# Key marks for four tokens an operation, and gates spread by two fp32r products, in a hybrid layer on one core

## The reference, cut to what matters

```python
def peer_block(h, w_query, sub_keys, expert_u, expert_v):
    ...
    cand_i = top_i[:, :, 0, :, None] * PEER_N_KEYS + top_i[:, :, 1, None, :]
    best_s, best_j = lax.top_k(cand_s.reshape(t, PEER_HEADS, PEER_TOPK * PEER_TOPK), PEER_TOPK)
    expert_idx = jnp.take_along_axis(cand_i.reshape(...), best_j, axis=-1)
    gate = jax.nn.softmax(best_s, axis=-1)
    act = jax.nn.gelu(jnp.einsum('td,thkd->thk', h, expert_u[expert_idx]), approximate=False)
    coef = (gate * act).astype(h.dtype)
    return jnp.einsum('thk,thkd->td', coef, expert_v[expert_idx])
```

## Time and profile before

| | |
|---|---|
| median of 3 runs | 3032.3 us (3028.78 to 3032.59) |
| the profiled execution's own time | 3030.53 us |
| its span in the trace | 3028.7 us |
| mean granted clock of TensorE | 0.932 of 2.4 GHz |
| PE busy | 2806.0 us, 93% |
| DVE busy | 1431.3 us, 47% |
| ACT busy | 911.8 us, 30% |
| POOL busy | 963.5 us, 32% |

### The profile page before, as it was taken

How to read it: one execution, slowest core, us unless ns; L and a number is a source line. 1 busy time by engine, 2 the same in 40 slices (tenths; PEclk the granted TensorE clock), 3 DMA queues, 4 the chain that set the end, 5 groups by cost and what they waited for, 6 DMA issues and landing times.

```text
span 3028.7 us, 41491 instructions
## 1 busy us (share of the span) xinstructions
PE 2806.0 (93%) x14216; PEld 2388.0 (79%) x14216; DVE 1431.3 (47%) x3468; ACT 911.8 (30%) x1205; POOL 963.5 (32%) x425
## 2 busy tenths in 40 slices
PE   8798898898899999769998999999999999999996
PEld 7688788788888677558877788888877888888885
DVE  2465565565565211244496677777502222222223
ACT  1412212212212132233332355545423222222221
POOL 0312302302302134324443333333344444444441
PEclk9897897897797999979999999999999999999998
DMA  4201101101100132213344345554665555555561
GB/s 184 71 28 42 55 14 42 55 17 38 55 28 28 56 111 90 91 60 111 111 131 129 104 160 176 208 169 160 215 207 180 183 181 200 180 188 193 174 203 53
DMA packets 130237, 354.27 MB, mean 117 GB/s; under 512 B 10640, under 2 KB 43536, under 8 KB 128784
## 3 DMA queue, kind: packets, MB, share of 16 engines
q1 hardware_dynamic: 127648, 312.76, 31.4%
q10 hardware_dynamic: 2544, 40.90, 3.5%
HBM read 284.41 MB, written 69.21 MB: 117 GB/s over the span
## 4 chain that ended last, share of the span: by engine, by line
issue 41%; PE 34%; POOL 17%; DVE 5%; ACT 2%; POOLq 0%; DMA 0%; DVEq 0%; SPq 0%; ACTq 0%
POOL w_lo L829 17%; PE bank L1355 5%; PE bank L466 4%; PE bank L467 4%; PE bank L468 4%; PE bank L1471 2%; DVE cv L1003 2%; PE bank L1486 2%; PE bank L1479 2%; PE bank L1414 1%; PE bank L1404 1%; PE bank L1595 1%; PE bank L1514 1%; PE bank L1446 1%; PE bank L1521 1%
## 5 line engine op out<-in xcount | busy, mean ns | idle before, releaser
L829 POOL TENSOR_TENSOR w_lo<-raw,w_hi 128x1024 fp32r<-128x1024 f32 x344 | 847.5, 2465 | 1768.1 <-ACT w_hi L698 868.8
L466 PE MATMUL bank<-lat_hi,w_hi 128*128 128x512 f32 x1568 | 631.8, 403 | 22.1 <-DMA sk<-sub_keys 8.0
L468 PE MATMUL bank<-lat_hi,w_lo 128*128 128x512 f32 x1568 | 615.1, 392 | 0.0
L467 PE MATMUL bank<-lat_lo,w_hi 128*128 128x512 f32 x1568 | 615.0, 392 | 0.0
L466 PE MATMUL bank<-c_hi,w_hi 128*128 128x512 f32 x1024 | 404.3, 395 | 7.0 <-ACT gu L755 7.0
L467 PE MATMUL bank<-c_lo,w_hi 128*128 128x512 f32 x1024 | 404.2, 395 | 0.0
L468 PE MATMUL bank<-c_hi,w_lo 128*128 128x512 f32 x1024 | 404.0, 395 | 0.0
L466 PEld LDWEIGHTS bank<-lat_hi,w_hi 128*128 128x128 f32 x1568 | 297.8, 190 | 82.1 <-issue 24.0
L468 PEld LDWEIGHTS bank<-lat_hi,w_lo 128*128 128x128 f32 x1568 | 296.8, 189 | 64.6
L467 PEld LDWEIGHTS bank<-lat_lo,w_hi 128*128 128x128 f32 x1568 | 297.7, 190 | 56.6
L1308 DVE TENSOR_SCALAR oh<-cst,eidT 128x128 f32<-128x128 f32 x512 | 242.6, 474 | 104.5 <-PE bank L1700 102.6
(11 more groups left out here) (283 smaller groups left out, 3572.6 us busy)
## 6 DMA issues: line engine op xcount, KB each, us to landing
raw<-w SPq DMA_DIRECT2D x344, 512.0 KB, 3.7
gu_dram<-gu SPq DMA_DIRECT2D x128, 256.0 KB, 3.9
g_dram<-gs ACTq DMA_DIRECT2D x8, 4096.0 KB, 12.4
gl<-gu_dram SPq DMA_DIRECT2D x32, 1024.0 KB, 6.8
gq<-g_dram SPq DMA_DIRECT2D x32, 1024.0 KB, 9.3
ada<-w_ada SPq DMA_DIRECT2D x32, 512.0 KB, 3.7
ada_a<-w_ada SPq DMA_DIRECT2D x12, 512.0 KB, 10.8
xin<-x SPq DMA_DIRECT2D x4, 512.0 KB, 12.4
```

Source lines behind the costliest of these rows:

```text
L466: nc.tensor.matmul(out, hi, rh, start=start, stop=False)
L467: nc.tensor.matmul(out, hi, rl, start=False, stop=False)
L468: return nc.tensor.matmul(out, lo, rh, start=False, stop=stop)
L829: nc.gpsimd.tensor_sub(w_lo[:, slot, :], raw[:, slot % RAW, :], w_hi[:, slot, :].bitcast(F32)).then_inc(split_done, 1)
```

## The change

The `oh` buffer becomes four: `oh_i` (marks of the first key, fp32r), `oh_j` (marks of the second key), `oh_h` (those marks times the gate's high part, fp32r) and `oh_l` (times the gate's low part, fp32r). Each has two buffers of four tokens. ACT makes the high part of all gates once (`g_hi`), and DVE subtracts it from row 2 of `eidT`. DVE makes the marks by tensor_tensor over four tokens at once. ACT multiplies by the high part, one activation with a scale for each token. PE does two fp32r products for a token in place of one fp32 product. DVE waits for each buffer by itself. ACT's copy out of the bank writes `gs` with the tokens innermost. ACT's outer loop has one turn less, and its last turn is written out.

```diff
-        oh = gates("oh", [2, 4, 2, P])
+        oh_i = gates("oh_i", [2, 4, P], F32R)
+        oh_h = gates("oh_h", [2, 4, P], F32R)
+        oh_l = gates("oh_l", [2, 4, P], F32R)
+        oh_j = gates("oh_j", [2, 4, P])
+        g_hi = gates("g_hi", [SEQ], F32R)
...
+            act.wait_ge(e_ev, LAT)
+            nc.scalar.copy(g_hi[:, :], eidT[:, 2, :]).then_inc(gh_done, 1)
+            def high_gates(n, group, z):
+                act.wait_ge(oh_second, n + (group + 1))
+                for v in range(4):
+                    nc.scalar.activation(oh_h[:, z, v, :], oh_j[:, z, v, :], ACT.Copy,
+                                         scale=g_hi[:, bass.ds(n * 4 + (4 * group + v), 1)].bitcast(F32)).then_inc(oh_high, 1)
+            act.wait_ge(gh_done, 1)
+            high_gates(0, 0, 0)
+            def gate_quarter(i, j, t, last):
+                for w in range(4):
+                    for z in range(2):
+                        n = i * (2 * GTOK // 4) + t * 8
+                        if not (last and w == 3 and z == 1):
+                            high_gates(n, j * GTOK // 4 + 2 * w + z + 1, 1 - z)
+                        act.wait_ge(g_mm, n + (j * GTOK // 4 + 2 * w + z + 1))
+                        nc.scalar.copy(gs[:, j, :, bass.ds(t * 32 + (8 * w + 4 * z), 4)],
+                                       bank[z][:, :].rearrange("p (t i) -> p i t", t=4)).then_inc(g_ev, 1)
...
-                                act.wait_ge(g_mm, i * (2 * GTOK // 4) + t * 8 + (j * GTOK // 4 + 2 * w + z + 1))
-                                nc.scalar.copy(gs[:, j, :, bass.ds(t * 32 + (8 * w + 4 * z), 4)].rearrange("p i t -> p t i"),
-                                               bank[z][:, :].rearrange("p (t i) -> p t i", t=4)).then_inc(g_ev, 1)
...
-            dve.wait_ge(e_ev, LAT)
-            with dve.Fori(0, SEQ // 8) as t:
+            dve.wait_ge(gh_done, 1)
+            g_lo = eidT[:, 2, :]
+            nc.vector.tensor_sub(g_lo, g_lo, g_hi[:, :].bitcast(F32)).then_inc(glo_done, 1)
+            dve.wait_ge(glo_done, 1)
+            def marks(t, z):
+                cols = bass.ds(t * 8 + 4 * z, 4)
+                nc.vector.tensor_tensor(oh_j[:, z, :, :], rep(iota, 4), bc(eidT[:, 1, cols], P), ALU.is_equal).then_inc(oh_second, 1)
+                nc.vector.tensor_tensor(oh_i[:, z, :, :], rep(iota, 4), bc(eidT[:, 0, cols], P), ALU.is_equal).then_inc(oh_first, 1)
+                dve.wait_ge(oh_second, t * 2 + (z + 1))
+                nc.vector.tensor_tensor(oh_l[:, z, :, :], oh_j[:, z, :, :], bc(eidT[:, 2, cols], P), ALU.mult).then_inc(oh_low, 1)
+            def marks_free(t, z):
+                dve.wait_ge(g_mm, t * 2 + (z + 1))
+                dve.wait_ge(oh_high, t * 8 + (4 * z + 4))
+                dve.wait_ge(oh_low, t * 2 + (z + 1))
+            for z in range(2):
+                marks(0, z)
+            with dve.Fori(0, SEQ // 8 - 1) as t:
                 for z in range(2):
-                    dve.wait_ge(g_mm, t * 2)
-                    for w in range(4):
-                        col = bass.ds(t * 8 + (4 * z + w), 1)
-                        first_ = oh[:, z, w, 0, :]
-                        nc.vector.tensor_scalar(first_, iota, eidT[:, 0, col], None, ALU.is_equal).then_inc(oh_done, 1)
-                        nc.vector.tensor_scalar(oh[:, z, w, 1, :], iota, eidT[:, 1, col], eidT[:, 2, col],
-                                                ALU.is_equal, ALU.mult).then_inc(oh_done, 1)
+                    marks_free(t, z)
+                    marks(t + 1, z)
...
-                        pe.wait_ge(oh_done, i * 64 + (16 * w + 8 * z + 8))
+                        pe.wait_ge(oh_high, i * 32 + (8 * w + 4 * z + 4))
+                        pe.wait_ge(oh_low, i * 8 + (2 * w + z + 1))
+                        pe.wait_ge(oh_first, i * 8 + (2 * w + z + 1))
...
-                            last = mm(bank[z][:, v * P:(v + 1) * P], oh[:, z, v, 1, :], oh[:, z, v, 0, :],
-                                      start=True, stop=True)
+                            out = bank[z][:, v * P:(v + 1) * P]
+                            mm(out, oh_h[:, z, v, :], oh_i[:, z, v, :], start=True, stop=False)
+                            last = mm(out, oh_l[:, z, v, :], oh_i[:, z, v, :], start=False, stop=True)
```

More of the change, by code:

```diff
@@ L413, in layer_kernel @@
         e_ev = sem("e_ev")
-        oh_done = sem("oh_done")
+        oh_first = sem("oh_first")
+        oh_second = sem("oh_second")
+        oh_high = sem("oh_high")
+        oh_low = sem("oh_low")
+        gh_done = sem("gh_done")
+        glo_done = sem("glo_done")
         g_mm = sem("g_mm")
@@ L776, in _, with gate_store @@
                 nc.scalar.copy(eidT[:, :, bass.ds(b * P, P)], bank[4][:, 0:3 * P].rearrange("p (a b) -> p a b", a=3)).then_inc(e_ev, 1)
-            with act.Fori(0, SEQ // GTOK // 2) as i:
+            act.wait_ge(e_ev, LAT)
[16 more added lines that the diff above has]
+                                       bank[z][:, :].rearrange("p (t i) -> p i t", t=4)).then_inc(g_ev, 1)
+                    x = i * (2 * GTOK // 8) + t * 4
+                    act.wait_ge(a_mm, x + (X_G + j * (GTOK // 8) + w + 1))
+                    act.wait_ge(gu_st[w % 2], x * 8 + (X_G + j * (GTOK // 8) + w) // 2 * 16)
+                    nc.scalar.activation(gu[:, w % 2, :], bank[6 + w % 2][:, :], ACT.Gelu).then_inc(gelu, 1)
+                    n = T_U + X_G - 2 * PH + j * (GTOK // 8) + RING + w
+                    act.wait_ge(raw_full[n % RAW], x * 8 + (n // 2 + 1) * 16)
+                    nc.scalar.copy(w_hi[:, n % RING, :], raw[:, n % RAW, :]).then_inc(hi_done, 1)
+            def gate_store(i, j):
+                act.wait_ge(g_ev, i * (2 * GTOK // 4) + (j + 1) * (GTOK // 4))
+                act.dma_start(g_dram[i * 2 + j], gs[:, j, :, :]).then_inc(gs_st[j], 16)
+            with act.Fori(0, SEQ // GTOK // 2 - 1) as i:
                 for j in range(2):
@@ L781, in _ @@
                     with act.Fori(0, GTOK // 32) as t:
-                        for w in range(4):
-                            for z in range(2):
-                                act.wait_ge(g_mm, i * (2 * GTOK // 4) + t * 8 + (j * GTOK // 4 + 2 * w + z + 1))
-                                nc.scalar.copy(gs[:, j, :, bass.ds(t * 32 + (8 * w + 4 * z), 4)].rearrange("p i t -> p t i"),
-                                               bank[z][:, :].rearrange("p (t i) -> p t i", t=4)).then_inc(g_ev, 1)
[L787 to L795, removed]
+                        gate_quarter(i, j, t, False)
+                    gate_store(i, j)
+            n_pair = SEQ // GTOK // 2 - 1
+            for j in range(2):
+                act.wait_ge(gs_st[j], n_pair * 16)
+                for t in range(GTOK // 32):
+                    gate_quarter(n_pair, j, t, j == 1 and t == GTOK // 32 - 1)
+                gate_store(n_pair, j)
             def act_c(i, y):
```

## The result

The changed kernel takes 3334.78 us (median of 4 runs, 3324.48 to 3337.0) against 3030.54 us, a ratio of 1.1003 with a 95% interval of 1.0972 to 1.1033. It is 304 us slower, where +180 us and a range of 3150 to 3280 us were forecast: the direction was right, the size wrong.

A forecast was written before the change was run, and what follows sets the result against it. PE was taken to bound the stage of products on marks. 3030.5 us plus 145 (longer rounds from the wait), 15 (table loads), 18 (clock) and 2 (start) gave 3210 us, range 3150 to 3280 us.

The forecast's parts named there:

- The place of the high parts in ACT's list: Behind Gelu and cast, they start 1.70 us after the round's beginning T; PE's second group starts at T + 3.12.
- The price of the four activations: ACT's four scaled 128-column activations for the second group take 1.30 us together, bounds 0.81 to 1.68 us.
- The price of a product on marks: Each narrow fp32r product on PE takes 0.11 us, 0.88 us a group of eight, so no gain on the product.
- the quick and the costly product: Rivals on PE's fp32r group: 0.45 us, 3183 us in all, chance 0.15; or 1.70 us, 3244 us, chance 0.22.
- The table loads: ACT table loads before PE's releaser delay 11 rounds by 1.38 us each, +15 us.
- Their clock charge: In the 11 rounds with a table load, PE's idling loses 1.7 us each to the half clock, +18 us.
- The step that failed is the clock: Plain rounds, with PE idle 2.2 us, keep the full clock, charge nothing; only table-load rounds lose, 18 us.
- A granted clock below 1.00 in the plain rounds: Sign that the forecast is wrong: the granted clock in rounds without a table load falls below 1.00.
- The rival: Plain rounds fall to the half clock too: +29 to +88 us, about 3240 to 3298 us, chance 0.15.
- DVE hidden: DVE's six tensor_tensors, 4.1 us, 6.5 with POOL's blocking, stay covered in a 9.56 us round.
- The copies hidden: ACT's copies out of the banks stay covered: its round is 6.3 us, each copy could take 1.5 us more.
- PE busy: Sign of the forecast: PE's busy share falls to about 75% in the stage of products on marks.

The follow-up runs named there:

- e1: The changed kernel with ACT's high parts of both buffers made right behind the copy of the same bank, ahead of the Gelu: 3024.58 us, ratio 0.9989.
- e7: e1 with the marks and both gate parts in bf16 instead of fp32r, high part made from the whole gate: 2987.13 us, ratio 0.986.
- e2: The changed kernel with nine unread fp32r products of 512 columns on PE while it waits for the second group's high parts: 3199.46 us.
- e4: The changed kernel with the second group's high parts between the Gelu and the cast, so PE waits less: 3217.61 us.
- e6: e4 with one fp32 product of marks and whole gates a token in place of two fp32r products: 3123.80 us.
- e9: e4 with 256 moving columns in place of 128 in each fp32r product on marks, gate table wrong: 3133.87 us.
- e8: The kernel before with DVE's part of the change alone, whole gates, fp32 products and ACT as before: 3025.87 us, ratio 0.9997.

## Why the prediction was wrong

- **The place of the high parts in ACT's list: right.** They started at T + 1.63 (forecast 1.70) and PE's second group at T + 3.14 (3.12). The idle time was 2.14 us (2.2). e1 shows that this place was the cause: with the high parts moved, the whole 304 us are gone.
- **The price of the four activations: right.** 1.28 us against 1.30.
- **The price of a product on marks: right at the full clock.** 0.11 us, 0.90 us a group; the quick and the costly product, the two rivals with 0.37 of the chance between them, did not happen. e7 shows that the quick one is real for bf16.
- **The table loads: right.** PE idles 3.50 to 3.60 us in 11 rounds, as many as forecast. Their clock charge was too low: they lose 2.5 us each (27 us) against 1.7 (18 us), measured as below.
- **The step that failed is the clock.** "The plain rounds idle 3.12 - 0.88 = 2.2 us, nearer to the latter, so I charge nothing there." Of the 51 counted, 49 fell to the half clock, for 6.8 us in the round shown, and it held for 44% of the stage. In total the clock cost 135 us (e2), not 18. The single rounds agree: against the 9.60 us and 10.96 us of e2's rounds without and with a table load, the changed kernel's plain rounds lose 115 us in all, where 0 was charged, and those with a load 27 us; e2 itself still loses 5 us in three of its rounds. A granted clock below 1.00 in the plain rounds was one of the prediction's own signs of being wrong. The rival was named, with a chance of 0.15, and would reach +88 us with 1.7 us in each of 52 rounds; 2.3 us were lost on average. I had compared idle times by length alone. The 1.97 us that did no harm came once, between long runs of products of 512 columns, 0.23 us apart; here the idle time comes in each round, between two groups of narrow products, 0.11 us apart, although 128 columns can follow each other in 0.055 us (e7). e4, e6 and e9 separate this: the same 1.2 us of idling costs 94 us of clock with fp32r products of 128 columns over what it costs with fp32 products (84 over those with 256 columns). That the idle time comes in each round does no harm by itself: e6 and e9 have it too, and lose nothing in their plain rounds.
- **A second thing was missed with it.** The second group runs behind the idle time, so it too ran at the half clock, 1.74 us in place of 0.9 in the round shown.
- **DVE hidden: right** (e8), though one of its operations takes 2.85 us in the round above, where the same operation alone takes 0.69. The Trainium skill, SBUF — State Buffer, Who interferes with whom, has it that a DVE instruction with two inputs in SBUF contends with a GpSimd one that reads SBUF; the trace agrees: POOL's operation of 2.45 us had begun 0.16 us before it.
- **The copies hidden: right.** They fell to 0.57 us from 1.12 with the tokens innermost, and nobody waited for them.
- **PE busy: near.** 80% in the stage (615.89 of 769 us), where 75% was forecast. One sum is off by 4 us: the forecast's own range comes to 3161 to 3252 us by its terms, not 3165 to 3250; nothing hangs on it.

The account: 307 us more in the stage are about 170 for the wait, table loads and start, and 135 for the clock. What stays open is how far the clock depends on the length of the idle time at each kind of product, and why rounds with the same idle time lose different amounts; three lengths (0, 1.2 and 2.1 us) by two kinds were run, the experiments with a wait once each.

## What to carry to other kernels

Before moving a step to an idle engine, look at what stands ahead of it in that engine's list: a step behind an instruction that waits for the bottleneck's last work can never be ready for its next work, however idle the engine is. An idle time on TensorE that comes back in each round can cost more than its length: here 1.2 us did so only with the narrow fp32r products around it, and 1.9 to 2.1 us with fp32 products as well. Filling it, or moving the step, gave the clock back too. Two fp32r products in place of one fp32 product gained nothing at 128 columns (e1), two bf16 products gained 1.4% of the kernel (e7): count the weight loads, and where the values allow it use bf16 for both parts.

## What the hardware did that I had not expected

- 1.2 us of idling a round brought the granted clock to 0.85 with fp32r products of 128 columns (e4), and left it at 0.99 with fp32 products that take as long (e6) and with fp32r products of 256 columns (e9). Without idling the narrow fp32r products kept 1.00 (e1).
- A fp32r product of 128 columns costs PE 0.11 us, and one of 256 columns 0.12 (e9); in bf16 it costs 0.055 us.
- A copy of 128 x 512 out of a bank took 0.57 us with its writes in runs of 16 bytes and its reads at a stride of 512 bytes, against 1.12 us with each 4-byte write 256 bytes from the last. Plain copies of that size (`sc`, L767 before) take 0.59 us, so the strided read costs nothing that shows, and the strided write doubles the time.
